# A routed expert layer on one core: each pair of items turned round, a fixed 64-slot item first, and the next item's units ahead of the scatter

## What is computed

```python
def moe(h, router, w_gate_up, w_down):
    B, S, D = h.shape
    xt = h.reshape(B * S, D)
    probs = jax.nn.softmax((xt @ router).astype(jnp.float32), axis=-1)
    top_p, top_i = lax.top_k(probs, TOP_K)
    top_p = top_p / jnp.sum(top_p, axis=-1, keepdims=True)
    gates = jnp.sum(jax.nn.one_hot(top_i, N_EXPERTS, dtype=jnp.float32) * top_p[..., None], axis=1)
    y = jnp.zeros_like(xt)
    for e in range(N_EXPERTS):
        y = y + gates[:, e:e + 1] * swiglu(xt, w_gate_up[e], w_down[e])
    return y.reshape(B, S, D)
```

## Time and profile before

| | |
|---|---|
| runs of the kernel before, median (lowest to highest) | 1146.75 us (1145.39 to 1146.88), 3 runs |
| the profiled execution, its own time | 1144.04 us |
| its span, first to last instruction | 1142.3 us |
| mean granted PE clock | 0.986 |
| PE busy / DVE / ACT | 94% / 55% / 46% of the span |
| read from HBM | 341.37 MB |

### The profile page before, as it was taken

The page is one execution under the profiler, slowest core; times in us unless marked ns, Lnnn a source line. Parts: engine busy times, 40 slices in busy tenths (PEclk is TensorE's granted clock), DMA queues, the critical chain, the costliest instruction groups (busy, mean ns, idle before and its releaser), DMA issues.

```text
span 1142.3 us, 15627 instructions
## 1 busy us (share of the span) xinstructions
PE 1079.3 (94%) x5708; PEld 799.8 (70%) x5708; DVE 626.5 (55%) x706; ACT 522.1 (46%) x571; POOL 22.3 (2%) x94
## 2 busy tenths in 40 slices
PE   7899999999999988999998999998999998999994
PEld 7877888888898777787355787355787455787441
DVE  6765555455654447896106896106896105897102
ACT  6554444344445643775015775005775004676001
POOL 2100000000000000000000000000000000000000
PEclk9899999999999997999999999999999999999998
DMA  9933456455454332998899999999999999999994
GB/s 350 346 116 111 149 183 203 168 192 210 148 185 147 115 107 97 364 359 318 320 415 409 404 417 409 361 415 410 404 415 409 367 413 411 404 416 408 356 413 182
DMA packets 110934, 343.46 MB, mean 301 GB/s; under 512 B 11613, under 2 KB 38282, under 8 KB 100618
## 3 DMA queue, kind: packets, MB, share of 16 engines
q1 hardware_dynamic: 110714, 341.93, 79.2%
q10 hardware_dynamic: 144, 0.52, 0.1%
HBM read 341.37 MB, written 1.05 MB: 300 GB/s over the span
## 4 chain that ended last, share of the span: by engine, by line
PE 80%; DMA 7%; DVE 5%; ACT 3%; issue 2%; SPq 2%; POOL 0%; POOLq 0%; ACTq 0%; DVEq 0%
PE ps L1484 21%; PE ps L1479 19%; PE ps L1481 19%; PE ps L1480 19%; DMA raw<-moe_w_gate_up_dram 5%; DMA raw<-moe_w_down_dram 2%; SPq L369 2%; ACT whi L558 2%; DVE wlo L958 1%; PE ps L1815 1%; DVE h L1212 1%; ACT xs L558 1%; PE ps L1494 1%; DVE h L1140 1%; PE ps L1859 1%
## 5 line engine op out<-in xcount | busy, mean ns | idle before, releaser
L558 ACT ACTIVATE whi<-raw 128x2048 fp32r<-128x2048 f32 (+1 forms) x195 | 335.8, 1724 | 241.2 <-PE ps L1481 223.9
L958 DVE TENSOR_TENSOR wlo<-raw,whi 128x2048 fp32r<-128x2048 f32 x151 | 345.4, 2291 | 120.5 <-ACT whi L558 119.6
L1479 PE MATMUL ps<-whi,xhi 128*128 128x512 f32 (+3 forms) x688 | 265.1, 385 | 17.4 <-DVE wlo L958 8.6
L1481 PE MATMUL ps<-wlo,xhi 128*128 128x512 f32 (+3 forms) x688 | 260.6, 379 | 0.0
L1480 PE MATMUL ps<-whi,xlo 128*128 128x512 f32 (+3 forms) x688 | 260.1, 378 | 0.0
L1479 PEld LDWEIGHTS ps<-whi,xhi 128*128 128x128 f32 x688 | 130.5, 190 | 45.9 <-issue 9.8
L1484 PE MATMUL ps<-raw,xs 128*64 128x512 f32 (+2 forms) x1024 | 155.0, 461 | 0.0
L1481 PEld LDWEIGHTS ps<-wlo,xhi 128*128 128x128 f32 x688 | 130.1, 189 | 24.1
L1480 PEld LDWEIGHTS ps<-whi,xlo 128*128 128x128 f32 x688 | 130.5, 190 | 22.3
L1484 PEld LDWEIGHTS ps<-raw,xs 128*64 128x64 f32 x1024 | 68.3, 137 | 81.6 <-issue 71.4
L1479 PE MATMUL ps<-whi,hhi 128*128 128x512 f32 x264 | 105.9, 401 | 0.0
(11 more groups left out here) (295 smaller groups left out, 949.5 us busy)
## 6 DMA issues: line engine op xcount, KB each, us to landing
raw<-moe_w_gate_up_dram SPq DMA_DIRECT2D x256, 512.0 KB, 13.0
raw<-moe_w_down_dram SPq DMA_DIRECT2D x80, 1024.0 KB, 17.1
raw<-moe_w_gate_up_dram SPq DMA_DIRECT2D x96, 384.0 KB, 9.4
raw<-ffn_w_gate_up_dram SPq DMA_DIRECT2D x44, 512.0 KB, 4.9
raw<-ffn_w_down_dram SPq DMA_DIRECT2D x22, 512.0 KB, 4.0
raw<-kv_shared_w_dram SPq DMA_DIRECT2D x16, 512.0 KB, 3.9
raw<-moe_w_gate_up_dram SPq DMA_DIRECT2D x32, 256.0 KB, 10.0
raw<-moe_w_down_dram SPq DMA_DIRECT2D x16, 512.0 KB, 17.9
```

The source lines that it names most:

```text
L558: return nc.scalar.activation(o, i, ACT.Copy, scale=scale)
L958: V.tensor_tensor(wlo[:, s, :].rearrange("p a w -> p (a w)"), raw[:, (hh // 2) % RAW, :], whi[:, s, :].bitcast(F32).rearrange("p a w -> p ...
L1479: pe.matmul(o, a_hi, b_hi, start=start, stop=False, skip_group_check=True)
L1481: return pe.matmul(o, a_hi, b_lo, start=False, stop=stop, skip_group_check=True)
```

## The change

Each pair is turned round: small first, big last. The first item is the fixed expert 3 (FIRST), small, fetched before the routing; of the other seven the three smallest are small and the four largest big. With the counts above there are again four pairs, the small items are again experts 3, 5, 1 and 2, and expert 0 is now the first of the big ones. The gather for a small item multiplies 64 columns of `sel` in place of 128. In `small`, PE now runs `begin` for the big item (two units) ahead of the scatter. Nothing is split ahead of the routing. The last item of all is big and has no gather, selection or `begin`. The overflow tables are simpler, so DVE has fewer small operations there. At the very start the gains' load stands between the two halves of x, PE transposes the gains first, ACT loads its table early, and attn_norm_0 is multiplied into x (two ACT and two DVE instructions of 256 columns per bank) and not into the weights.

```diff
-ORDER = (0, 1, 5, 2, 6, 3, 7, 4) + OVF * (-1,)
+FIRST = 3
+ORDER = (0, 4, 1, 5, 2, 6, 3, 7) + OVF * (-1,)
...
             sp_eng.wait_ge(items_ready, 2)
             for p in range(PAIRS - 2):
-                small_loads(p, at(2 * p + 1), lambda x: after_big(x, p))
-                big_loads(p + 1, at(2 * p + 2), lambda x: after_small(x, p))
+                big_loads(p, at(2 * p + 1), lambda x: after_small(x, p))
+                small_loads(p + 1, at(2 * p + 2), lambda x: after_big(x, p))
...
-            x_high(0, banks=[0])
+            act.wait_ge(ident_ready, 1)
+            copy(table_scratch[:, :], ident[:, 0:1])
             act.wait_ge(g_tr, 1)
             copy(gcol[:, 0:KD], ps[:, 7, 0:KD]).then_inc(g_ready, 1)
...
+            for b in range(4):
+                x_high(0, G_ATTN0, banks=[b])
+                split_high(b)
+            for hh in range(4, 8):
                 split_high(hh)
...
                 for j in range(1, SMALL_GROUPS):
                     gate(j)
-                if following == "big":
-                    gathered_low(p + 1)
+                gathered_low(p)
+                for x in range(2):
+                    split_low_unit(H_MOE + 2 * x, p)
                 dve.wait_ge(small_used, p * FU + FU)
                 V.tensor_copy(ys[:, :], ps[:, 4, :]).then_inc(ys_ready, 1)
-                if following == "big":
-                    for x in range(3):
-                        split_low_unit(H_MOE + 2 * x, p + 1)
+                for x in range(2, 4):
+                    split_low_unit(H_MOE + 2 * x, p)
                 add_in(g)
-                if following == "big":
-                    for x in range(3, 5):
-                        split_low_unit(H_MOE + 2 * x, p + 1)
+                split_low_unit(H_MOE + 2 * 4, p)
...
-            def gather(g):
+            def gather(g, slots):
...
-                        last = mm(o, xm[:, c, k * P:(k + 1) * P], sel[:, c, :], c == 0 and k % 4 == 0, c == TC - 1)
+                        last = mm(o, xm[:, c, k * P:(k + 1) * P], sel[:, c, 0:slots], c == 0 and k % 4 == 0, c == TC - 1)
...
-            gather(0)
-            selection("big", 0)
-            begin("big", 0, 0)
+            gather(0, SMALL)
+            begin("small", 0, 0)
+            selection("small", 0)
             for p in range(PAIRS - 2):
-                big(p, 2 * p, "small", p)
-                small(p, 2 * p + 1, "big", p + 1)
+                small(p, 2 * p, p)
+                big(p, 2 * p + 1, "small", p + 1)
...
-            big(final, 2 * final, "small", final)
-            small(final, 2 * final + 1, None, None)
+            small(final, 2 * final, final)
+            big(final, 2 * final + 1, None, None)
```

More of the change, by code:

```diff
@@ L126, in gain_of @@
 def gain_of(h):
[L129 removed]
+    for first, last, g, chunks in ((H_UQ, H_UKV, G_Q, 3), (H_UKV, H_WO, G_KV, 2),
                                    (H_SBK, H_SBQ, G_KVSH, KD), (H_SBQ, H_SBV, G_ATTN1, KD), (H_SBV, H_SBO, G_KVSH, KD)):
@@ L402, in small_loads, with tokens @@
                     item_unit(x, *w)
-            for n in range(2):
+            def tokens(n):
                 w = slice(n * 512, (n + 1) * 512)
@@ L819, in small @@
                 hidden(3)
-                if following is None:
-                    act.dma_start(gbc, t["final_norm"].partition_broadcast(P)).then_inc(gbc_in, 16)
-                if following == "big":
[L823 to L827, removed]
-                if following == "big":
-                    for x in range(5):
-                        split_high_unit(H_MOE + 2 * x, p + 1, g + 1)
+                gathered_high(p, g + 1)
+                transposed(g + 1)
+                for x in range(5):
+                    split_high_unit(H_MOE + 2 * x, p, g + 1)
             x_high(1, G_FFN0)
@@ L885, in _ @@
             softplus_part(1)
-            for m in range(4):
+            for m in range(2):
                 split_high(H_SBO + RING + m)
@@ L902, in _ @@
             nc.scalar.activation(den[:, :], best[:, :], ACT.Exp).then_inc(gap_exp, 1)
-            gathered_high(0, 0)
+            gathered_small(0)
             transposed(0)
-            for x in range(3, 5):
-                split_high_unit(H_MOE + 2 * x)
             for p in range(PAIRS - 2):
-                big(p, 2 * p, "small")
-                small(p, 2 * p + 1, "big")
+                small(p, 2 * p)
+                big(p, 2 * p + 1, "small")
             act.wait_ge(items_ready, 2)
@@ L913, in _ @@
             with act.Fori(PAIRS - 2, final) as p:
[L914 to L917, removed]
+                small(p, 2 * p)
+                big(p, 2 * p + 1, "small")
+            small(final, 2 * final)
+            big(final, 2 * final + 1, None)
             n_items = 2 * final + 2
@@ L1246, in big, with small @@
                         gate({7: 1, 15: 3, 21: 5}[x])
-                    if x == 29 and following == "big":
-                        gathered_low(i + 1)
-                if following == "big":
-                    for x in range(3, 5):
-                        split_low_unit(H_MOE + 2 * x, i + 1)
                 add_in(g)
-            def small(p, g, following):
+            def small(p, g):
                 def gate(j):
@@ L1450, in _ @@
             V.memset(table_scratch[:, :], 0.0).then_inc(h_ready[4], 4)
-            for x in range(3, 5):
-                split_low_unit(H_MOE + 2 * x)
             for p in range(PAIRS - 2):
-                big(p, 2 * p, "small")
-                small(p, 2 * p + 1, "big")
+                small(p, 2 * p)
+                big(p, 2 * p + 1, "small")
             dve.wait_ge(items_ready, 2)
@@ L1882, in small @@
                         transposes(d + 1)
-                    if d == 5 and following is not None:
+                    if d == 5:
                         pe.wait_ge(hT_ready, p * SMALL_GROUPS + SMALL_GROUPS)
-                        gather(g + 1)
-                    if d == 8 and following is not None:
-                        selection(following, next_i)
-                if following is not None:
-                    pe.wait_ge(selN_ready, g + 2)
+                        gather(g + 1, P)
+                    if d == 8:
+                        selection("big", next_i)
+                begin("big", next_i, g + 1)
+                pe.wait_ge(selN_ready, g + 2)
                 pe.wait_ge(ys_ready, p + 1)
```

160 lines of the change are left out of this document (65 added, 95 removed).

## The result

| | before | changed |
|---|---|---|
| median on one chip, 4 runs each | 1146.07 us (1144.63 to 1146.88) | 1151.98 us (1151.01 to 1154.12) |
| the profiled execution: own time, span | 1144.04, 1142.3 | 1152.49, 1150.7 |
| mean granted PE clock | 0.986 | 0.979 |

The ratio is 1.0055, 95% interval 1.0041 to 1.007: slower by half a per cent. Forecast were 1142.0, faster by 0.4%, a range of 1135 to 1150, and a chance of 0.15 for slower. The measured time lies above the range, and the change went the other way.

A forecast was written before the change was run, and what follows sets the result against it. Bound: a loop of landing, big item on PE, first release by the small item, stream, next landing. First landing 503.0, three loops of 172.9, last item 101.8, 2.0, 12.7, start -0.5: span 1137.7, 4.6 less, about 1142.0; range 1135 to 1150.

The forecast's parts named there:

- Together +0.5 per pair: Small to big: scatter behind two units adds 2.0 us, PE's wait for DVE at the fourth unit saves 1.5.
- first slot free at 440.9: Start of the items: PE goes on at 439.1 at full clock, and a 1.8 us small unit frees the slot.
- the gain of 64 columns at 0: Small items' gathers: columns do not set the pace, so 64 cost what 128 do, 3.7 us.
- I take 62.0: First small item's stream, first issue to next big item's first landing: 62.0 us, between 61.2 and 64.05.
- rival 2: Stream refills slowly in the first small item: first landing 8.6 us later, half likelier, +4.3, 1146.5; chance 0.12.
- the loop is 172.4 + 0.5 = 172.9: Each of three loops between big items' first landings: 172.4 us before, 0.5 more for the new order.
- the forecast's own sign: Stated test: wrong if the loop differs by over 1 us from 172.9, or PE waits inside the first small item.
- The last item is big ... 101.8: Last big item has no gather, selection or wait at it: 106.8 - 5.0 = 101.8 us, ending at 1123.5.
- The very start, -0.5: First product, with gains transposed first and table loaded early: 0.5 us gained, ends -1 and +0.5.
- 1 (the gather shrinks): Gathers do get shorter with 64 columns: 3.1 less in the first, 1.9 in each of three loops, 1133; chance 0.10.
- 3 (VectorE falls behind): At small to big the addition ends late and PE waits 2.7 us in each of four pairs, 1153; chance 0.10.
- 4: An expert counted over 64 among the small ones forces an extra pair: +172, 1314; chance 0.01.

The follow-up runs named there:

- filler14: Changed kernel plus 14 unread 512-column products on PE between each small item and the next big one: 1145.66 us, ratio 0.9998 to the kernel before.
- before_units_first: Kernel before, with only the next big item's first two units moved ahead of the small item's scatter, VectorE's order to match: 1151.73 us, ratio 1.0063.
- units_first_full_clock: Changed kernel, own order, plus 14 products between small and big, 5, 8 and 3 in the routing's idle time, 128-column gathers: 1141.96 us, ratio 0.9963.
- change_again: The changed kernel unaltered, run again on another chip: 1153.77 us, ratio 1.0064 to the kernel before.
- scatter_first: Changed kernel with the small item's scatter again ahead of the big item's first two units, VectorE's old order: 1144.43 us, ratio 0.9992.
- before_new_start: Kernel before with only the changed kernel's very start: 1144.88 us, ratio 0.9997.
- wide_gather: Changed kernel with all gathers over 128 columns in place of 64 for small items: 1151.01 us, ratio 1.0057.
- scatter_first_wide: scatter_first with all gathers over 128 columns: 1141.57 us, ratio 0.9959.
- scatter_wide_again: scatter_first_wide repeated unaltered, beside scatter_wide_filled on the same chip: 1141.13 us, ratio 0.9957.
- scatter_first_filled: scatter_first plus 5, 8 and 3 unread 512-column products in TensorE's idle time of the routing: 1142.95 us, ratio 0.9967.
- scatter_wide_filled: scatter_first_wide plus the routing's unread products of scatter_first_filled: 1139.98 us, ratio 0.9949.
- before_filled: Kernel before plus the routing's unread products of scatter_first_filled: 1142.63 us, ratio 0.9973.

## Why the prediction was wrong, point by point

- **"PE's start is set by the landing (landing + 4.36), so the wait and scatter ahead of it were covered by the DMA and their removal gains nothing. The scatter now lies behind two units, on the path: +2.0 ... So -1.5. Together +0.5 per pair."** This is the step that failed. Landing, split, product, scatter and VectorE's queue came as counted; what was left out is that the scatter divided PE's idle time. Moved away it leaves 4.5 us in one piece, the clock falls, and units 0 and 1 take 7.2 to 8.5 in place of 5.7: 1.5 + 2.7 + 1.6 + 1.5 = 7.3 us. filler14 and before_units_first show it, one by taking it away and one by making it. I had read the same in the routing, where PE ran at 0.50 after its idle time, and used it only there. The Trainium skill ("TensorE: Matmul & The Clock Gate", HAM oscillation) describes a kernel in which the wait for DMA ahead of each tile throttles PE anew every time. The trace agrees: 4.5 us idle (here for a landing and the two splits behind it), then a clock of 0.50 to 0.52 in the windows above. It should have been a rival.
- **"without that idle time I take full clock", first slot free at 440.9.** Wrong by 2.35. The removal of the idle time at 439 was right (PE went on at 439.52), but the clock had been at half since 426, and the gather of 64 columns, at full busy share, did not bring it back. "I put the gain of 64 columns at 0" was right for the pass (3.68 against 3.73) and left out what hangs on it, the clock: some 3 us with the scatter first, nothing that the times show in the changed kernel's own order.
- **The first stream, "I take 62.0" between 61.2 and 64.05.** The upper end was right: from the first issue, 443.25, to the split, 507.30, is 64.05; the nine other profiles with a small first item have 63.1 to 64.3. So I took the wrong end, 2.0 of the miss. Windows of the changed kernel:

```profile
447.00:451.00 4.00, 4.00 (x22) 1.39 (x20) 0.00 (x0) 0.07 (x1) 0.00 (x0) 1.00 0.96 323
451.00:455.00 4.00, 4.00 (x22) 1.34 (x20) 0.00 (x0) 0.00 (x0) 0.00 (x0) 1.00 1.01 404
...
460.00:470.00 10.00, 10.00 (x48) 3.34 (x48) 0.00 (x0) 0.54 (x1) 0.00 (x0) 1.00 1.05 394
```

  The stream takes some 8 us from the first issue to come near its steady rate: rival 2 at a quarter of its full price.
- **"the loop is 172.4 + 0.5 = 172.9."** 174.8, 176.0, 174.9: by the forecast's own sign (over 1 us from 172.9) this was wrong. Less the clock's 1.5, 2.7 and 1.6 they are 173.2 to 173.3 each, and 173.0 to 173.5 in units_first_full_clock: apart from the clock right to 0.6. But the stream alone can add more, since two loops of filler14 at full clock have 174.3 and 174.8.
- **"The last item is big ... 101.8", +2.0, +12.7.** 101.9 at full clock, 103.4 in the change; 2.01 and 12.4. Right, and the load of final_norm was hidden.
- **The very start, -0.5.** Not there: 0.2 at the first product, and a longer time at half clock behind it.
- **Rivals.** 1 (the gather shrinks): no, 3.68 against 3.73. 3 (VectorE falls behind): no, PE never waited at a big item's third to fifth unit. 4: no, four pairs. The range's top, 1150, fell short by 2 us, since no case in it took the clock away for a move of instructions.

## What to carry to other kernels

An instruction that seems free because it runs inside another wait may be what keeps TensorE's clock up; before it is moved, add up the idle time that is left in one piece and look for the clock in a stretch of the same trace with as long a gap. Where such a gap can't be closed, products whose result nobody reads can hold the clock: 14 of them did here in all eight places of two profiles, and PE's first product stood 4.36 us behind the split with and without them. And price a filling stream by a measured one of the same shape, not by its steady rate.

## What was unexpected of the hardware

- A stretch in which PE was busy throughout, 7.06 us of fp32 products with 64 columns, ran at half clock from end to end. At full clock the same 32 passes take 3.68. In the routing half clock lasted 17.1 us in the three profiles with that gather and no fillers there (change, change_again, scatter_first), 20.5 in filler14, and 10.2 to 13.7 in the six with 128 columns (before, before_units_first, before_new_start, wide_gather, scatter_first_wide, scatter_wide_again; the first two have another 3.4 at the first big units, behind an idle time of 2.4, which before_new_start has, too, without that loss).
- The idle time of 4.5 us or more cost the clock in all 15 places of four profiles, for 3.4 us in some and 6.8 in others of the same kernel (1.5 and 2.7 us of time in the change). Idle times of 0.8 and 1.8 to 2.4 us with the scatter of 2.0 between them cost it in 5 places, although neither was as long.
- The same fillers in the routing left half clock for 3.4 us in two profiles (scatter_first_filled, scatter_wide_filled), for 6.8 and another 3.4 at the first units in before_filled, and for 10.2 in units_first_full_clock. What decides between them no run tells.
